# TensorE's expert loop at a given slot of an instruction-fetch block, with its far jumps announced

## The chip, the cores and the metric

One core of a Trainium2 chip runs the whole program. The metric is the device time of one execution in microseconds (us). Every core has five instruction streams (TensorE, VectorE, ScalarE, GpSimd, SyncE) that meet only at semaphores, and 16 DMA engines. A stream is fetched from memory in blocks while it runs; those fetches are DMA packets of their own, and the page of the profile lists them by queue as "instruction".

## The reference, cut to what matters

A decoder layer in float32: 256 tokens, 2048 channels. Attention, a gated mixer and an output projection come first. The part around the change is the second half, a mixture of 16 experts in 4 groups; every token goes to two experts of one group.

```python
    for e in range(N_EXPERTS):
        hid = jax.nn.silu(t @ w_gate[e]) * (t @ w_up[e])
        y = y + combine[:, e:e + 1] * (hid @ w_down[e])
```

How many tokens an expert gets is known only at run time.

## The kernel before

The program starts with the attention and mixer part, written out flat, up to about 850 us of the span. Then come the experts, four to a turn, in a loop of four turns. Each of TensorE, ScalarE, VectorE and SyncE has its own loop over the turns.

TensorE's turn: it gathers the tokens of the turn's four experts (64 places each) with matmuls of `hot` against `x1` (helper at line 924). Then, for each of the four experts `le`, it loads the expert's token count into a register (`value_load`, helper at line 1213) and asks whether it exceeds 64 (`br_cond`, line 628). If not, it goes on in the next instructions, the small body `pe{le}_few`. If so, it jumps to `pe{le}_more`, which lies behind the whole loop, asks again (line 640 and below) and runs one of three large bodies: `one_extra` (up to 96 tokens), `two_extra` (up to 128) or `all_extra`. The large body repeats the expert's work with further tiles of tokens: a gather of these tokens (line 741), turns (lines 694 and 756), gate and up products (line 675), down products (line 687) and sums (line 699). Its last instruction jumps back to `pe{le}_end` in the middle of the loop (lines 644, 651 and the one after). The large bodies are placed behind the loop in the order of the experts, each as a copy of its own.

Every float32 matmul of the source is four instructions of TensorE's stream (two weight loads, two matmuls; the profile counts the pairs). With that, the stream ahead of the loop has 7,175 instructions. Counted from the loop's first instruction as 0, the question of expert 0 is instruction 136, `pe0_end` begins at 553, `pe2_end` (where the count of the last expert is loaded) at 1466, the jump back is 1960, `pe0_more` is 1962, `one_extra` of expert 0 goes from 1963 to 3274, and its `two_extra` from 3276 to 5470, each with the jump out as its last instruction.

The weights of an expert are 12 transfers of 2048 KB. SyncE issues them in the order of use into seven places, each when TensorE's last matmul from that place is done (`half_multiplied` and `load_half`, lines 562 to 573). When all seven are full, the DMA engines stand still until TensorE frees one.

VectorE adds the results into `acc`; after the last expert it normalises, and SyncE stores the output.

Of the kernel before, what the change touches and what calls it, by code (L numbers as in the profile page):

```python
# [26 lines left out]
NE = 16  # L27
# [12 lines left out]
EXTRA = {1: (64, 32, 2), 2: (96, 32, 3), 3: (128, 64, 4), 4: (192, 64, 7)}  # L40
GRP = 4
# [43 lines left out]
def fills(n):  # L85

    return n // RING - sum(m <= n and m % RING == n % RING for m in ODD_ROWS)
# [46 lines left out]
def expert_at(g, le):  # L134

    return le % GRP * GRP + g + le // GRP
# [33 lines left out]

E_PLACES = 7
TURN_HALVES = 2 * GRP * E_UNITS

def place_of(t, h):

    return (2 * t + h) % TURN_HALVES % E_PLACES

LAST_USE = [max(range(i, TURN_HALVES, E_PLACES)) for i in range(E_PLACES)]

def uses(i):

    return len(range(i, TURN_HALVES, E_PLACES))

# [4 lines left out]
def program(nc, x_tok_d, x_T_d, c_T_d, rel_bias_d, router_w_d, router_b_d, ada_w_d, ada_b_d, ada_bT_d, w_in_d,  # L192
            sgu_g_d, sgu_b_d, sgu_wT_d, sgu_bias_d, w_branch_d, w_out_d, ln1_g_d, ln1_b_d, ln2_g_d, ln2_b_d,
            w_up_gate_d, w_down_d, square_d, slots_d, buckets_d, out_d):
    with ExitStack() as ctx:
# [227 lines left out]
        def e_half_loaded(eng, g, t, h):  # L423

            i, use = place_of(t, h), (2 * t + h) // E_PLACES
            before = 0 if i == E_PLACES - 1 else fills(NFRONT + i // 2) - 1
            eng.wait_ge(expert_landed(t, h), g * (16 * uses(i)) + 16 * (before + use + 1))

        def expert_half(t, h):

            i = place_of(t, h)
            if i == E_PLACES - 1:
                return region_g[:, :]
# [24 lines left out]
        def _(sp):  # L458
# [122 lines left out]
            with sp.Fori(0, NE // GRP - 1) as g:  # L581
                for i in range(E_PLACES, TURN_HALVES):
                    half_multiplied(g, (i - E_PLACES) // 2, (i - E_PLACES) % 2)
                    load_half(g, i // 2, i % 2)
                for i in (E_PLACES - 1, *range(E_PLACES - 1)):
                    half_multiplied(g, LAST_USE[i] // 2, LAST_USE[i] % 2)
                    load_half(g, GRP * E_UNITS + i // 2, i % 2)
            for i in range(E_PLACES, TURN_HALVES):
                half_multiplied(NE // GRP - 1, (i - E_PLACES) // 2, (i - E_PLACES) % 2)
# [32 lines left out]
                return four[c][:, a * 256:(a + 1) * 256]  # L622
            return four[2 * a + c][:, :]

        def few_tokens(eng, name, count, body):

            here = nc.cur_bb
            eng.br_cond(count > EXTRA[1][0], on_true=f"{name}_more", on_false=f"{name}_few")
            nc.switch_bb(f"{name}_few", parent=here)
            body(())  # L630
            eng.br(f"{name}_end")
            nc.switch_bb(f"{name}_end", parent=here)
            return here

        def more_tokens(eng, name, kind, count, here, body):

            more = nc.body(f"{name}_more", parent=here, valid_engines=[kind])
            with more:
                above = nc.cur_bb
                eng.br_cond(count > EXTRA[2][0], on_true=f"{name}_over_two", on_false=f"{name}_one_extra")  # L640
                nc.switch_bb(f"{name}_one_extra", parent=above)
                body((1,))
                eng.sem_inc(extra_end[kind], 1)
                eng.br(f"{name}_end")
                nc.switch_bb(f"{name}_over_two", parent=above)
                above = nc.cur_bb
                eng.br_cond(count > EXTRA[3][0], on_true=f"{name}_all_extra", on_false=f"{name}_two_extra")
                nc.switch_bb(f"{name}_two_extra", parent=above)
                body((1, 2))
                eng.sem_inc(extra_end[kind], 1)  # L650
                eng.br(f"{name}_end")
                nc.switch_bb(f"{name}_all_extra", parent=above)
                body((1, 2, 3, 4))
                eng.sem_inc(extra_end[kind], 1)
                eng.br(f"{name}_end")

        def bank_of(x, n):
            return psum[n] if x == 0 else psum[EXTRA[x][2]]
# [263 lines left out]
        def _(pe):  # L922
            def mm(out, lhsT, rhs, start, stop):
                return nc.tensor.matmul(out, lhsT, rhs, start=start, stop=stop)  # L924
# [270 lines left out]

            pe.wait_ge(routed, 1)
            with nc.Fori(0, NE // GRP, engines=[mybir.EngineType.PE], hint_back_edge=True) as g:

                pe.wait_ge(hot_ready, g + 1)  # L1200
                for m in range(KC // 2):
                    b = m % len(SUM_BANKS)

                    pe.wait_ge(m_taken[b], g * BANK_JOBS + m // len(SUM_BANKS) + 1)
                    for kk in range(2):
                        k = 2 * m + kk
                        for a in range(TT):
                            last = mm(psum[SUM_BANKS[b]][:, kk * T:(kk + 1) * T], x1[:, a, k * P:(k + 1) * P],
                                      hot[:, a, :, :].rearrange("p e s -> p (e s)"), a == 0, a == TT - 1)
                    last.then_inc(m_full[b], 1)  # L1210
                asked = []
                for le in range(GRP):
                    count = pe.value_load(counts[0:1, bass.ds(expert_at(g, le), 1)], min_val=0, max_val=T)
                    here = few_tokens(pe, f"pe{le}", count, lambda xs: expert_pe(pe, mm, g, le, xs))
                    asked.append((count, here))
            for le, (count, here) in enumerate(asked):
                more_tokens(pe, f"pe{le}", mybir.EngineType.PE, count, here, lambda xs: expert_pe(pe, mm, g, le, xs))

# [788 lines left out]
```

## Time and profile before

| | us |
|---|---|
| median of 3 runs | 1926.54 (1922.68 to 1928.22) |
| the profiled execution | 1924.21 |
| its span, first to last instruction | 1922.5 |
| TensorE matmuls busy | 1752.0 (91%) |
| DMA, mean rate over the span | 328 GB/s |
| VectorE busy | 508.8 (26%) |

The span is cut by turns: the flat part to 850, the first turn to 1142, the second to 1404, the third to 1639, the fourth to 1900, then the last normalisation. In a busy figure for TensorE a matmul that waits inside the array or runs at half clock counts as busy, so 91% doesn't say that TensorE is the limit everywhere. "issue" as the cause of idle time means that the engine waited for nothing that the profile shows: its own instruction stream hadn't delivered the next instruction. "GB/s" of a stretch shows whether the weights flow (428 is what they reach when nothing holds them) or stand.

### The profile page before, as it was taken

Reading aid. Unit: us, or ns where it says so; the run is one execution under the profiler, and the core shown is the slowest. Engines: PE = TensorE matmul, PEld = TensorE weight load, DVE = VectorE, ACT = ScalarE, POOL = GpSimd, SP = SyncE. Lnnn points to the kernel's source line nnn. Section 1 sums busy time; section 2 is a strip of 40 time slices with the busy share of each in tenths; the row PEclk is TensorE's granted clock in tenths of the full one; section 3 lists DMA queues with packets and bytes.
Section 4 is the critical chain, followed back from the end, with each engine's and each line's share of the span. In section 5 each row is a group of like instructions: output and inputs, shape, how many; then the busy total and the mean of one; then the engine's idle time right before and its main releaser. Section 6 shows DMA issues by size and latency. Waiting matters only on the chain.

```text
span 1922.5 us, 21633 instructions
## 1 busy us (share of the span) xinstructions
PE 1752.0 (91%) x8982; PEld 957.5 (50%) x8983; DVE 508.8 (26%) x944; ACT 163.5 (9%) x342; POOL 2.5 (0%) x9
## 2 busy tenths in 40 slices
PE   6889999999999999978989988899899888899994
PEld 3337888688888884454433243333243222432321
DVE  1441436655355101140121120111111111111114
ACT  0001013100000000041000011000020000200000
POOL 0000000000000000000000000000000000000000
PEclk9889999999999999989999998999999999999998
DMA  9996884687668624433779996899999999699995
GB/s 385 425 392 175 348 351 183 257 333 328 271 274 345 263 109 176 175 132 125 277 304 429 427 427 279 363 412 428 427 429 428 429 427 429 289 408 374 427 428 215
DMA packets 50993, 629.65 MB, mean 328 GB/s; under 512 B 5775, under 2 KB 8240, under 8 KB 11848
## 3 DMA queue, kind: packets, MB, share of 16 engines
q1 hardware_dynamic: 49768, 623.15, 78.2%
q10 hardware_dynamic: 1120, 5.00, 0.7%
q8 instruction: 78, 1.28, 0.3%
q14 instruction: 27, 0.22, 0.0%
HBM read 624.46 MB, written 3.67 MB: 327 GB/s over the span
## 4 chain that ended last, share of the span: by engine, by line
PE 76%; DMA 16%; DVE 3%; issue 2%; SPq 1%; ACT 1%; ACTq 0%; DVEq 0%
PE bank L924 42%; PE bank L675 20%; PE bank L687 9%; DMA ring<-in_w_down 8%; DMA ring<-in_w_up_gate 7%; PE bank L699 3%; DMA ring<-in_w_in 1%; DVE ada_rows L1534 1%; PE bank L694 1%; PE bank L741 1%; SPq L470 1%; PE bank L956 1%; ACT region_f L1226 0%; DVE region_a L1493 0%; SPq L463 0%
## 5 line engine op out<-in xcount | busy, mean ns | idle before, releaser
L675 PE MATMUL bank<-ring,region_b 128*64 128x512 f32 x1792 | 410.0, 606 | 39.5 <-DMA ring<-in_w_up_gate 18.5
L924 PE MATMUL bank<-region_a,ring 128*128 128x256 f32 x1792 | 390.3, 380 | 0.0
L924 PEld LDWEIGHTS bank<-region_a,ring 128*128 128x128 f32 x1792 | 340.1, 190 | 48.8 <-issue 3.8
L675 PEld LDWEIGHTS bank<-ring,region_b 128*64 128x64 f32 x1792 | 125.8, 139 | 298.3 <-issue 265.3
L687 PE MATMUL bank<-ring,region_f 128*64 128x512 f32 (+1 forms) x1408 | 231.0, 518 | 31.6 <-DMA ring<-in_w_down 25.1
L1534 DVE SCALAR_TENSOR_TENSOR ada_rows<-ring,condT,ada_rows 128x512 f32<-128x512 f32 x293 | 220.2, 752 | 10.2 <-DMA ring<-in_ada_w 0.3
L687 PEld LDWEIGHTS bank<-ring,region_f 128*64 128x64 f32 (+1 forms) x1408 | 78.3, 127 | 168.4 <-issue 121.8
L1855 DVE TENSOR_TENSOR region_a<-bank,region_a 128x512 f32<-128x512 f32 x128 | 79.5, 683 | 204.3 <-PE bank L699 202.9
L924 PE MATMUL bank<-ring,region_b 128*128 128x512 f32 x256 | 110.3, 593 | 1.3 <-issue 1.3
L924 PE MATMUL bank<-ring,region_a 128*128 128x512 f32 x160 | 76.0, 629 | 7.6 <-DMA ring<-in_w_in 6.8
L924 PEld LDWEIGHTS bank<-ring,region_b 128*128 128x128 f32 x256 | 48.5, 190 | 61.9 <-issue 61.9
L1860 DVE TENSOR_TENSOR sgu_wT<-bank,g2x 128x512 f32<-128x512 f32 x32 | 22.1, 691 | 207.7 <-PE bank L687 207.6
L1882 DVE TENSOR_TENSOR work<-work,bank 128x256 f32<-128x256 f32 x32 | 13.5, 421 | 230.5 <-ACT work L1275 230.5
L924 PE MATMUL bank<-region_f,ring 128*128 128x256 f32 x256 | 60.9, 393 | 3.0 <-DVE region_d L1632 3.0
L675 PE MATMUL bank<-region_g,region_b 128*64 128x512 f32 x256 | 58.1, 596 | 4.9 <-DMA region_g<-in_w_up_gate 4.9
L924 PE MATMUL bank<-region_e,region_x 128*128 128x256 f32 x256 | 58.1, 389 | 3.8 <-DVE region_e L1775 2.9
L924 PE MATMUL bank<-region_d,ring 128*128 128x256 f32 x256 | 57.9, 379 | 0.0
L1275 ACT ACTIVATE work<-bank 128x256 f32<-128x256 f32 x32 | 12.3, 383 | 521.1 <-PE bank L675 521.1
L924 PEld LDWEIGHTS bank<-region_e,region_x 128*128 128x128 f32 x256 | 49.7, 195 | 13.2 <-DVE region_a L1855 3.3
L924 PEld LDWEIGHTS bank<-region_f,ring 128*128 128x128 f32 x256 | 50.6, 199 | 10.9 <-issue 3.7
L924 PEld LDWEIGHTS bank<-ring,region_a 128*128 128x128 f32 x160 | 31.4, 203 | 45.3 <-issue 37.6
L924 PEld LDWEIGHTS bank<-region_d,ring 128*128 128x128 f32 x256 | 48.7, 190 | 6.6
(180 smaller groups left out, 862.3 us busy)
## 6 DMA issues: line engine op xcount, KB each, us to landing
ring<-in_w_up_gate SPq DMA_DIRECT2D x112, 2048.0 KB, 21.8
ring<-in_w_down SPq DMA_DIRECT2D x56, 2048.0 KB, 20.8
ring<-in_ada_w SPq DMA_DIRECT2D x44, 2048.0 KB, 11.8
ring<-in_w_in SPq DMA_DIRECT2D x31, 2048.0 KB, 16.3
region_g<-in_w_up_gate SPq DMA_DIRECT2D x16, 2048.0 KB, 22.5
ring<-in_w_branch SPq DMA_DIRECT2D x8, 2048.0 KB, 17.9
ring<-in_w_out SPq DMA_DIRECT2D x8, 2048.0 KB, 11.4
region_g<-in_w_down SPq DMA_DIRECT2D x8, 2048.0 KB, 21.8
```

The costliest lines, as they stand in the source:

```text
L470: sp.dma_start(dst[:, :, cols], w_in_d[first:first + width, :, cols].rearrange("u p n -> p u n"))\
L675: last = nc.tensor.matmul(bank_of(x, j)[n * c:n * c + n, 0:2 * m], tokens(x, 8 * half + k), w[:, k % 4, :, m * c:m * c + m], start=(half = ...
L687: last = nc.tensor.matmul(bank_of(x, q)[n * c:n * c + n, 0:m], hidT[x][:, k, :], w[:, k % 4, m * c:m * c + m], start=(k == 0), stop=(k == ...
L694: last = nc.tensor.transpose(psum[5][:, b * P:(b + 1) * P], src[:, b * P:(b + 1) * P], ident)
L699: return nc.tensor.matmul(bank, ones_t[n * c:n * c + n, a, :], y[n * c:n * c + n, :], start=True, stop=True, tile_position=(n * c, 0))
L741: last = nc.tensor.matmul(own[n * c:n * c + n, :], hotx[:, a, 0:n], x1[:, a, col:col + 512], start=(a == 0), stop=(a == TT - 1), tile_posi ...
L924: return nc.tensor.matmul(out, lhsT, rhs, start=start, stop=stop)
L956: last = nc.tensor.matmul(psum[6][32 * c:32 * c + 32, :], cond_pad[:, 32 * k:32 * k + 32], w[:, k, :], start=(k < 4), stop=(k >= KC - 4), ...
L1534: ins = dve.scalar_tensor_tensor(out=dst, in0=w[:, k, :], scalar=condT[:, k:k + 1], in1=dst, op0=ALU.mult, op1=ALU.add)
L1855: return dve.tensor_tensor(dst, bank[:, :], dst, ALU.add)
L1860: dve.tensor_tensor(ysb[q], psum[q][:, :], g2x[:, q * UW:(q + 1) * UW], ALU.mult)\
L1882: dve.tensor_tensor(hid[j], silu_g[j], psum[j][:, 256:512], ALU.mult).then_inc(hid_ready, 1)
```

## The change

A constant `LOOP_SLOT = 104` is added. In place of `Fori`, TensorE's loop is written by hand: a register counts the turns, an `addr_align` puts the instruction behind the next jump on slot 104 of a fetch block, and the back jump is a compare-and-branch. Five kinds of jump in TensorE's stream are announced: at the start of a turn the question of expert 0 (before, the back jump was announced there); at the start of each large body its jump out; ahead of loading the last expert's count the jump back. `few_tokens` takes the announcement of its question, and `leave` attaches one to the jump out. Other engines keep their code; matmuls, waits and their order stay.

```diff
+LOOP_SLOT = 104
...
+            jump = eng.br_cond(count > EXTRA[1][0], on_true=f"{name}_more", on_false=f"{name}_few")
+            if announced is not None:
+                jump.branch_hint(announced)
...
+        announcing = (mybir.EngineType.PE,)
+
+        def leave(eng, label, announced):
+
+            jump = eng.br(label)
+            if announced is not None:
+                jump.branch_hint(announced)
...
                 nc.switch_bb(f"{name}_one_extra", parent=above)
+                announced = eng.mark_branch_hint_location() if kind in announcing else None
                 body((1,))
                 eng.sem_inc(extra_end[kind], 1)
-                eng.br(f"{name}_end")
+                leave(eng, f"{name}_end", announced)
...
-            with nc.Fori(0, NE // GRP, engines=[mybir.EngineType.PE], hint_back_edge=True) as g:
+            kinds = [mybir.EngineType.PE]
+            turn_no = nc.alloc_registers("expert_turn", engines=kinds)
+            nc.regs_mov(turn_no, 0)
+            pe.addr_align(bass.FETCH_BLOCK_INSTRUCTIONS, offset=LOOP_SLOT, max_nops=0)
+            nc.br("pe_expert_turn", engines=kinds)
+            with nc.body("pe_expert_turn", valid_engines=kinds):
+                g = nc.snap(turn_no, min_val=0, max_val=NE // GRP - 1)
+                large_announced = pe.mark_branch_hint_location()
...
+                    if le == GRP - 1:
+                        back_announced = pe.mark_branch_hint_location()
...
+                nc.regs_alu(turn_no, turn_no, 1, op=mybir.AluOpType.add)
+                pe.br_lt(turn_no, NE // GRP, on_true="pe_expert_turn", on_false="pe_experts_end").branch_hint(back_announced)
+            nc.switch_bb("pe_experts_end")
```

The same announcement stands at the start of `two_extra` and `all_extra`.

## Rows read from the trace of the kernel before

**Rows 1.** The page: the chain that ended last, and the instruction packets of queue 8.

```profile
PE 76%; DMA 16%; DVE 3%; issue 2%; SPq 1%; ACT 1%; ACTq 0%; DVEq 0%
q8 instruction: 78, 1.28, 0.3%
```

**Rows 2.** Windows by turn: PE, PEld, DVE, ACT, POOL busy; clock, DMA share, GB/s.

```profile
850.00:1142.00 292.00, 265.30 (x1800) 105.82 (x1800) 49.84 (x108) 23.66 (x51) 0.00 (x0) 0.97 0.75 311
1142.00:1404.00 262.00, 237.32 (x1361) 89.66 (x1360) 41.03 (x83) 20.29 (x44) 0.00 (x0) 0.97 0.92 386
1404.00:1639.00 235.00, 206.99 (x921) 73.54 (x920) 32.58 (x66) 18.29 (x38) 0.00 (x0) 1.00 1.01 428
1639.00:1900.00 261.00, 236.22 (x1361) 89.38 (x1360) 40.08 (x75) 20.30 (x44) 0.00 (x0) 0.98 0.90 378
```

**Rows 3.** Waits of TensorE in 1404:1639 (us in total, times, longest).

```profile
PE bank L687 <- DMA ring<-in_w_down: 11.3, 10, 1.3
```

**Rows 4.** Timeline of TensorE, second turn, first matmuls of the large body.

```profile
1157.98 0.43 PE L694 MATMUL bank<-square,region_e 128*128 128x128 f32 x2 [1.39 <-ACT region_b L1447]
1159.16 0.14 PEld L741 LDWEIGHTS bank<-region_x,region_e 128*32 128x32 f32 x2 [0.98 <-issue]
1159.17 0.61 PE L741 MATMUL bank<-region_x,region_e 128*32 128x512 f32 x1 [0.75 <-ACT region_d L1266]
1165.80 3.64 PE L741 MATMUL bank<-region_x,region_e 128*32 128x512 f32 x15 [6.02 <-issue]
1169.36 4.08 PE L675 MATMUL bank<-ring,region_b 128*64 128x512 f32 x16
```

**Rows 5.** The same place in the fourth turn.

```profile
1662.28 3.35 PE L741 MATMUL bank<-region_x,region_e 128*32 128x512 f32 x15 [5.63 <-issue]
1665.55 3.65 PE L675 MATMUL bank<-ring,region_b 128*64 128x512 f32 x16
```

**Rows 6.** Timeline of TensorE, first turn, jumps into the large body.

```profile
873.19 0.61 PE L694 MATMUL bank<-square,region_e 128*128 128x128 f32 x2 [4.74 <-issue]
874.55 3.64 PE L741 MATMUL bank<-region_x,region_e 128*32 128x512 f32 x16 [0.75 <-ACT region_d L1266]
```

**Rows 7.** Timeline of TensorE at the jumps out: turns one, two, four.

```profile
981.80 5.70 PE L675 MATMUL bank<-ring,region_b 128*64 128x512 f32 x16 [5.46 <-issue]
...
1243.50 6.25 PE L675 MATMUL bank<-ring,region_b 128*64 128x512 f32 x16 [3.94 <-issue]
...
1739.28 5.35 PE L675 MATMUL bank<-ring,region_b 128*64 128x512 f32 x16 [3.96 <-issue]
```

**Rows 8.** Timeline of TensorE at a jump back, the one ahead of turn three.

```profile
1399.37 4.92 PE L699 MATMUL bank<-sgu_wT,ada_rows 64*128 64x512 f32 x16
1404.63 14.08 PE L924 MATMUL bank<-region_e,region_x 128*128 128x256 f32 x64 [0.35 <-issue]
```

**Rows 9.** Instruction packets (count, MB): 0:850, 1142:1150, 1238:1404, 1404:1658.

```profile
q8 instruction: 28, 0.46, 0.2%
...
q8 instruction: 1, 0.02, 0.8%
...
q8 instruction: 7, 0.11, 0.3%
...
q8 instruction: 1, 0.02, 0.0%
```

**Rows 10.** Windows: clock behind a stall; DMA around three exits and a body's start.

```profile
1166.00:1170.00 4.00, 4.00 (x17) 0.73 (x11) 0.00 (x0) 0.51 (x1) 0.00 (x0) 0.50 0.19 74
...
982.00:994.00 12.00, 12.00 (x46) 3.67 (x46) 2.49 (x6) 0.00 (x0) 0.00 (x0) 0.84 0.50 190
1244.00:1258.00 14.00, 14.00 (x54) 4.29 (x52) 2.48 (x4) 0.00 (x0) 0.00 (x0) 0.83 0.71 286
1741.00:1753.00 12.00, 12.00 (x52) 3.90 (x50) 2.48 (x4) 0.00 (x0) 0.00 (x0) 0.89 0.75 294
1166.00:1182.00 16.00, 16.00 (x133) 5.88 (x129) 1.38 (x2) 2.26 (x3) 0.00 (x0) 0.87 0.05 20
```

More of the change, by code:

```diff
@@ L623, in sum_bank, with few_tokens @@
             return four[2 * a + c][:, :]
-        def few_tokens(eng, name, count, body):
+        def few_tokens(eng, name, count, body, announced=None):
             here = nc.cur_bb
-            eng.br_cond(count > EXTRA[1][0], on_true=f"{name}_more", on_false=f"{name}_few")
+            jump = eng.br_cond(count > EXTRA[1][0], on_true=f"{name}_more", on_false=f"{name}_few")
+            if announced is not None:
+                jump.branch_hint(announced)
             nc.switch_bb(f"{name}_few", parent=here)
@@ L648, in more_tokens @@
                 nc.switch_bb(f"{name}_two_extra", parent=above)
+                announced = eng.mark_branch_hint_location() if kind in announcing else None
                 body((1, 2))
                 eng.sem_inc(extra_end[kind], 1)
-                eng.br(f"{name}_end")
+                leave(eng, f"{name}_end", announced)
                 nc.switch_bb(f"{name}_all_extra", parent=above)
+                announced = eng.mark_branch_hint_location() if kind in announcing else None
                 body((1, 2, 3, 4))
                 eng.sem_inc(extra_end[kind], 1)
-                eng.br(f"{name}_end")
+                leave(eng, f"{name}_end", announced)
         def bank_of(x, n):
@@ L1212, in _ @@
                 for le in range(GRP):
+                    if le == GRP - 1:
+                        back_announced = pe.mark_branch_hint_location()
                     count = pe.value_load(counts[0:1, bass.ds(expert_at(g, le), 1)], min_val=0, max_val=T)
-                    here = few_tokens(pe, f"pe{le}", count, lambda xs: expert_pe(pe, mm, g, le, xs))
+                    here = few_tokens(pe, f"pe{le}", count, lambda xs: expert_pe(pe, mm, g, le, xs),
+                                      large_announced if le == 0 else None)
                     asked.append((count, here))
+                nc.regs_alu(turn_no, turn_no, 1, op=mybir.AluOpType.add)
+                pe.br_lt(turn_no, NE // GRP, on_true="pe_expert_turn", on_false="pe_experts_end").branch_hint(back_announced)
+            nc.switch_bb("pe_experts_end")
             for le, (count, here) in enumerate(asked):
```

## The prediction

> **What bounds the kernel now.** Start at the chain of the page: TensorE has 76% of it, the DMA engines 16%, and "issue" 2% [rows 1]. Two per cent are small, but they are the only time that this change can touch, so I looked for where they lie. The windows by turn tell which engine sets the pace: in the third turn the weights flow at 428 GB/s, their full rate, and TensorE waits for them in small pieces (10 waits for the down weights, 11.3 us); in the first, second and fourth they flow at 311, 386 and 378 [rows 2, 3]. Those three turns have a large body for expert 0 (the timeline shows lines 741 and 694 there: `two_extra` in the first turn, `one_extra` in the second and fourth). In a large body TensorE is so slow with a set of weights that all seven places fill and the DMA engines stand: 20 GB/s in 1166:1182 [rows 10]. From there until the places empty again, a microsecond lost by TensorE is lost at the end; once the weights flow at full rate, TensorE's losses are covered by the waits for weights.
>
> The timeline of TensorE then shows the stalls by "issue" in those stretches: 4.74 us on the way into the first large body, 6.02 and 5.63 us inside the other two, and 5.46, 3.94 and 3.96 us at the three jumps out; at a jump back only 0.35 [rows 4 to 8]. [...]
>
> **What the stalls are.** The flat part has 7,175 instructions and 28 packets: 256 to a block [rows 9]. In the second turn 16 instructions of the large body run (three register or wait instructions, the two pairs of line 694 with their waits and registers, two weight loads and one matmul of line 741), then nothing for 6.02 us [rows 4]. So a block begins at instruction 1979 of the loop. 1979 + 69 = 2048 = 8 x 256: the loop's head now lies at slot 69, the loop fills eight blocks to slot 2029, and `pe0_more` with 16 instructions of the body is the tail of the eighth. The third turn needs one packet in 1404:1658 [rows 9], so at least eight blocks are kept. Behind the exit of turn two come 7 packets and then that one: all eight blocks anew, the head's among them, and still the jump back costs 0.35 us [rows 8, 9]. So the announcement works, and it works late: the head's block is asked for when the block with the announced jump is entered, in place of the block that follows. This is also why the body's second block is missing at instruction 1979: the armed word named the head. From asking to going on takes 5.6 to 6.0 us, by the two stalls inside the bodies.
>
> **Part by part.** New places: head at slot 104, one more instruction by then (the announcement ahead of the last expert), so the jump back is at 104 + 1961 = 2065, slot 17 of a ninth block, and `pe0_more` at slot 19 of it.
>
> 1. *The second block of the body.* It is now 236 instructions behind the jump in, and the next block is asked for on entering the ninth. The 6.02 and 5.63 us go. With them goes the half clock: the 15 gather matmuls take 3.64 and 3.35 us, about 1.8 at full clock, and line 675 has 4.08 against 3.65 in turn two: 2.2 and 1.5 us. DMA stands behind both [rows 10], so all of it counts: 8.2 + 7.1 = 15.3.
>
> 2. *The exits.* The jump out of `two_extra` lies 201 instructions behind its block's start: hidden. Of 5.46 us some 0.8 for loading the count remain, so 4.7 + 2.05 of clock = 6.75. In `one_extra` it lies 52 instructions behind the start of its block (of 1313, from slot 20). Those 52 run in about 4.4 us and are issued ahead, so of the 3.94 us some 0.8 remain; if nothing were issued ahead, 2.7. Middle: 3.1 + 2.6 = 5.7 and 3.1 + 1.7 = 4.8. But what comes next is the weights: they can gain only the time in which they stand around the exit, by the windows 12 x (1 - 190/428) = 6.7, 14 x (1 - 286/428) = 4.6 and 12 x (1 - 294/428) = 3.8 us [rows 10]. The exits give 6.7 + 4.6 + 3.8 = 15.1.
>
> 3. *The question at the turn's start.* It matters in the first turn alone: afterwards the ninth block is there from the turn before. Announced, the first of two fetches goes. Without that fetch the second starts while the gathers still run, and of 4.74 us about 1.6 remain (in turn two, with no fetch at all, 1.39 at this place [rows 4]): 3.1. On the way the ninth block's follower is asked for as well and may hold up the jump to `two_extra`, by nothing or by as much as the 3.1; no row shows which, and I take 0.8 off, nearer to nothing, because a fetch that nobody waits for needn't be first. Half clock: 16 matmuls in 3.64 us [rows 6] and the next ones, some 2.5. Together 4.8; between 0 (the jump lies in the block in which it is announced, which no row shows to work) and 5.6.
>
> 4. *The jump back.* It lies 17 instructions behind the ninth block's start. If the head's block is still there, 0 are lost. If not, it is asked for only then. The last instructions are issued while the 16 matmuls of line 699 run (4.92 us, to 1404.3) [rows 8]: asked for about 1400.3, there at 1406.2, 1.9 us lost; asked for only as its matmuls run (1402.4), 4.0. No row shows whether nine blocks are kept. I take 1.9, as issue runs ahead elsewhere too. Ahead of turn three it is hidden (weights flow on at 428); ahead of two and four it counts: 3.8. The bounds are 0 and, unannounced, 5.7 + 2.2 of clock each.
>
> [...]
>
> 5. *Added instructions*: an announcement per turn and body, once a jump over at most 255 empty slots ahead of the loop, which costs no more than a jump back does, 0.35 us [rows 8]. Nothing that counts. No queue of DMAs is moved.
>
> **Sum.** 15.3 + 15.1 + 4.8 - 3.8 = 31.4 us. Profiled execution: 1924.2 - 31.4 = 1892.8. The median of the runs lies 2.3 above that execution; I state 1893.
>
> **Rivals.**
> - *A jump back with no time to announce* (fetched at full price, 7.9 instead of 1.9 twice): 12 more, 1905. For it: only 17 instructions. Against: issue ahead. 0.14.
> - *The exits' announcements do nothing*, say because they hold only for a compare-and-branch, and what is announced here is an unconditional jump: 15.1 are missing, 1908. No row shows one announced. 0.12.
> - *None of the announcements acts* (the change doesn't do what it says) and only the place counts: bodies -15.3, two jumps back + 15.8: 1924.7, no change. Against: the announcement of before worked. 0.05.
> - *Slower: an announcement takes the turn of the block that follows it.* It stands just behind a block's start in every large body. Then the body's next block is missed again in turns two and four (no gain), newly in the first (+8.1), and the block behind the last expert's start four times at 8.1 less some 4.8, four waits for weights of 1.2 us [rows 3] that cover it (+13.2); the exits of turns two and four still gain 8.4 and the first question 4.8: +8.1, 1932. It decides once the dropped fetch costs more than the waits behind it. Against: at the head of turn two the announcement came at once behind a block's start and that block's follower was still fetched (1 packet in 1142:1150) [rows 9]. 0.05.
> - *Smaller gains by mixtures of these*: 0.09, between 1897 and 1918.
>
> **How the numbers follow.** My forecast has 0.55, with its own range 1886 (no loss at the jumps back, all of item 3, 1 us of noise) to 1900 (item 3 at nothing, exits at their lower end). To hold 8 in 10, the range takes in the first two rivals: 1885 to 1911. Faster by over 0.3% (5.8 us, about what a measurement can tell): 0.55 + 0.14 + 0.12 + 0.07 = 0.88; within: 0.07; slower: 0.05.
>
> **What would show it.** In the timeline of after: the 15 matmuls of line 741 follow the first without a gap (item 1); no gap over 1 us and 16 matmuls in 3.65 us behind each exit, and the weights' windows there near 428 (item 2); the gap ahead of line 694 in turn one at about 1.5 (item 3); gaps of about 2 us ahead of the gathers of turns two to four (item 4); and instruction packets in the third turn: one if nine blocks are kept, eight or nine if not. Wrong would be: a long gap at another instruction of a large body, or a half clock behind the jumps back.

## The result and the profile after

The changed kernel takes 1915.84 us (median; 1913.61 to 1919.88) where the kernel before takes 1927.26 beside it: ratio 0.9949, 95% interval 0.9936 to 0.9961. It is faster by some 10 us (0.0051 of 1927; the two medians differ by 11.4), where 31.4 were forecast, and outside the range of 1885 to 1911. The profiled execution of after takes 1914.61 us, its span is 1912.8; before had 1924.21 and 1922.5. In the code of after the lines have moved: 675 is now 689 (gate and up), 687 is 701 (down), 694 is 708, 699 is 713 (sums), 741 is 755 (the body's gather), 924 is 938 (the turn's gather), 640 is 651.

The page of after, its chain and its instruction packets [answers to rows 1]:

```profile
q8 instruction: 85, 1.39, 0.3%
...
PE 76%; DMA 16%; DVE 3%; issue 2%; SPq 1%; ACT 1%; ACTq 0%; DVEq 0%
```

Seven packets more, and still 2% "issue". The windows by turn, cut at the first gather matmul of each turn [rows 2]:

```profile
852.40:1140.10 287.70, 262.33 (x1801) 105.03 (x1801) 50.41 (x102) 22.38 (x50) 0.00 (x0) 0.98 0.78 326
1140.10:1399.20 259.10, 237.00 (x1361) 90.81 (x1361) 41.13 (x82) 20.28 (x44) 0.00 (x0) 0.97 0.92 389
1399.20:1639.60 240.40, 208.13 (x921) 74.67 (x921) 32.47 (x64) 18.29 (x38) 0.00 (x0) 0.99 0.99 420
1639.60:1900.00 260.40, 234.60 (x1360) 90.13 (x1360) 46.57 (x86) 20.87 (x46) 0.00 (x0) 0.98 0.88 368
```

For the same cut of before, the timeline of TensorE has its first gathers at these times (the third turn's is in [rows 8]):

```profile
852.57 1.64 PE L924 MATMUL bank<-region_e,region_x 128*128 128x256 f32 x3 [2.91 <-DVE region_e L1775]
...
1142.51 1.77 PE L924 MATMUL bank<-region_e,region_x 128*128 128x256 f32 x7 [0.34 <-issue]
...
1639.38 1.99 PE L924 MATMUL bank<-region_e,region_x 128*128 128x256 f32 x8 [0.20 <-issue]
```

From first gather to first gather, and in the fourth turn to TensorE's last sum (1899.45 before, 1889.98 after), the turns took 289.9, 262.1, 234.8 and 260.1 us; now they take 287.7, 259.1, 240.4 and 250.4. Three turns gained; the third, which has no large body, lost 5.6. The timeline of after tells why. These are the gathers ahead of turns two, three and four:

```profile
1140.10 2.50 PE L938 MATMUL bank<-region_e,region_x 128*128 128x256 f32 x5 [6.32 <-issue]
...
1399.17 2.07 PE L938 MATMUL bank<-region_e,region_x 128*128 128x256 f32 x4 [6.16 <-issue]
...
1639.57 6.80 PE L938 MATMUL bank<-region_e,region_x 128*128 128x256 f32 x19 [6.42 <-issue]
```

A jump back that cost 0.2 to 0.35 us now costs 6.2 to 6.4, all three times. The rest of the change did what it should. First the question of turn one and the first matmuls of the large bodies of turns two and four [rows 4 to 6], then the first matmuls behind the three exits [rows 7]:

```profile
871.56 0.43 PE L708 MATMUL bank<-square,region_e 128*128 128x128 f32 x2 [3.30 <-issue]
...
1159.83 3.60 PE L755 MATMUL bank<-region_x,region_e 128*32 128x512 f32 x16 [0.83 <-ACT region_d L1293]
...
1658.66 1.92 PE L755 MATMUL bank<-region_x,region_e 128*32 128x512 f32 x16 [0.75 <-ACT region_d L1293]
1660.52 3.65 PE L689 MATMUL bank<-ring,region_b 128*64 128x512 f32 x16
```

```profile
974.40 3.65 PE L689 MATMUL bank<-ring,region_b 128*64 128x512 f32 x16 [0.93 <-issue]
...
1232.95 3.60 PE L689 MATMUL bank<-ring,region_b 128*64 128x512 f32 x16
...
1730.11 3.60 PE L689 MATMUL bank<-ring,region_b 128*64 128x512 f32 x16
```

The 16 matmuls of line 755 run without a gap. In turn four they take 1.92 us; in turn two they take 3.60, at a granted clock of 0.53 in 1159.8:1163.4, so a half clock stands there still, without a stall ahead of it. Behind all three exits 16 matmuls take 3.60 to 3.65 us. Windows of after (clock, DMA share and GB/s are the last three columns): around the exits, behind the first jump back, and in the third turn:

```profile
975.00:987.00 12.00, 12.00 (x58) 4.00 (x56) 4.80 (x9) 0.00 (x0) 0.00 (x0) 1.00 0.99 400
1232.00:1246.00 14.00, 14.00 (x66) 4.62 (x64) 3.87 (x8) 0.00 (x0) 0.00 (x0) 1.00 1.00 421
1730.00:1742.00 12.00, 12.00 (x56) 3.90 (x54) 3.78 (x7) 0.00 (x0) 0.00 (x0) 1.00 1.00 417
...
1140.00:1143.00 3.00, 2.90 (x7) 2.37 (x8) 0.05 (x1) 0.00 (x0) 0.00 (x0) 0.50 1.01 423
...
1415.00:1425.00 10.00, 8.88 (x42) 3.18 (x44) 0.00 (x0) 2.06 (x3) 0.00 (x0) 1.00 0.60 233
```

Around the exits the weights flow at 400 to 421 GB/s where they had 190 to 294 [rows 10]. Behind the jump back the clock is 0.50. And the fifth window shows something that the prediction had excluded: in the third turn, some 16 us behind the stall, the weights fall to 233 GB/s for 10 us. Through the stall itself they flowed on (426 GB/s in 1133.5:1139.5 of the first jump back), so the places filled while TensorE emptied none. SyncE's waits for a free place there show it, after (1385:1430) and before (1404:1430), in total, times and longest:

```profile
SPq L574 <- PE bank L689: 36.2, 3, 30.6
...
SPq L573 <- PE bank L675: 26.1, 2, 23.3
```

Packets of queue 8 of after, in 866:869 and 1399:1640, and below them those of before in 866:870:

```profile
q8 instruction: 2, 0.03, 8.6%
...
q8 instruction: 9, 0.15, 0.2%
```

```profile
q8 instruction: 1, 0.02, 1.5%
```

Nine packets in the third turn, as many as the loop has blocks. Two packets at once at the first question: their share, 8.6% of 16 engines in 3 us, is 4.1 us, or 2.1 us for each, against 1.5% of 4 us, 0.96 us, for the single one of before.

### The profile page after: what moved, and what is told of

It is laid out like the page before. It is cut to its first block, busy times and chain, and to the rows that moved or that the text cites. A ratio compares the mean times of both kernels' runs of the same rounds, so it can differ in the third digit from the quotient of the medians.

```text
span 1912.8 us, 21645 instructions
## 1 busy us (share of the span) xinstructions
PE 1747.9 (91%) x8982; PEld 959.1 (50%) x8983; DVE 508.8 (27%) x944; ACT 163.4 (9%) x342; POOL 2.5 (0%) x9
## 4 chain that ended last, share of the span: by engine, by line
PE 76%; DMA 16%; DVE 3%; issue 2%; SPq 1%; ACT 1%; ACTq 0%; DVEq 0%
PE bank L938 42%; PE bank L689 20%; PE bank L701 9%; DMA ring<-in_w_down 8%; DMA ring<-in_w_up_gate 7%; PE bank L713 3%; DMA ring<-in_w_in 1%; DVE ada_rows L1561 1%; PE bank L708 1%; SPq L471 1%; PE bank L970 1%; PE bank L755 1%; ACT region_f L1253 0%; DVE region_a L1520 0%; SPq L464 0%
## 5 line engine op out<-in xcount | busy, mean ns | idle before, releaser
L689 PE MATMUL bank<-ring,region_b 128*64 128x512 f32 x1792 | 402.4, 596 | 30.6 <-DMA ring<-in_w_up_gate 22.1
L938 PE MATMUL bank<-region_e,region_x 128*128 128x256 f32 x256 | 65.0, 421 | 21.8 <-issue 18.9
L1909 DVE TENSOR_TENSOR work<-work,bank 128x256 f32<-128x256 f32 x32 | 13.5, 421 | 237.4 <-ACT work L1302 237.4
L938 PEld LDWEIGHTS bank<-region_e,region_x 128*128 128x128 f32 x256 | 54.5, 215 | 33.3 <-issue 24.4
## 6 DMA issues: line engine op xcount, KB each, us to landing
ring<-in_w_down SPq DMA_DIRECT2D x56, 2048.0 KB, 22.2
ring<-in_w_branch SPq DMA_DIRECT2D x8, 2048.0 KB, 18.2
region_g<-in_w_down SPq DMA_DIRECT2D x8, 2048.0 KB, 23.3
```

The source lines that it names most:

```text
L689: last = nc.tensor.matmul(bank_of(x, j)[n * c:n * c + n, 0:2 * m], tokens(x, 8 * half + k), w[:, k % 4, :, m * c:m * c + m], start=(half = ...
L1909: dve.tensor_tensor(hid[j], silu_g[j], psum[j][:, 256:512], ALU.mult).then_inc(hid_ready, 1)
```

## The experiments

Two theories stood at the beginning. Mine: an announced block is asked for on entering the block that holds the jump, and the jump back of after comes too soon behind that (slot 18 of the ninth block, counted in the program; the prediction had 17). The rival: the stall has another cause than the distance, such as a hand-written jump that is not served as the `Fori`'s was, or a ninth block that is too much. Positions below are slots of 256-instruction blocks: with the head at slot s, the jump back lies at s + 1962, the question of expert 0 at s + 137, the exits of `one_extra` and `two_extra` of expert 0 at s + 3277 and s + 5474.

**The head at slot 84**, where the jump back lies in the eighth block.

```diff
-LOOP_SLOT = 104
+LOOP_SLOT = 84
```

> The changed kernel with LOOP_SLOT = 84 instead of 104 and nothing else. The loop then ends with the jump back at slot 254 of its eighth block, and the first large body starts the ninth. In the changed kernel the gap ahead of the gathers of turns two to four is 6.2 us each and no packet is asked for between the start of the ninth block and the jump, 18 slots later. Theory 'too late': an announced block is asked for when the block with the jump is entered, and a jump that comes before the packet has gone out asks anew and pays the whole price; then the three gaps shrink to about 0.35 and the kernel gains about 5.8 us for each, so about 1897 to 1900. Theory 'without effect': the announcement ahead of the last expert does nothing wherever the jump lies; the head's block has been pushed out by the ninth, and the gaps stay at 6. By both the jump out of one_extra, now 33 slots behind its block's start instead of 53, may become a gap of up to 3.9 us again (1905 to 1908 in that case).

Measured: 1917.42 us (ratio 0.995, interval 0.9935 to 0.9965), no better than after. Ahead of turn three:

```profile
1399.00 1.22 PE L938 MATMUL bank<-region_e,region_x 128*128 128x256 f32 x2 [6.42 <-issue]
```

All three stalls stay, at 6.4 to 6.5 us, though the jump lies 254 slots behind its block's start. "Distance from the block's start" alone is therefore wrong or incomplete; the last experiment comes back to it.

**The head at slot 160**: the jump back at slot 74 of the ninth block.

```diff
-LOOP_SLOT = 104
+LOOP_SLOT = 160
```

> The changed kernel with LOOP_SLOT = 160: the jump back lies 74 slots behind the start of the ninth block, the loop still needs nine blocks. 'Too late': with 74 slots the head's block comes in time, and the gaps ahead of turns two to four fall from 6.2 to below 1 us, though nine blocks don't fit. 'Without effect': they stay at 6.2. A third theory, that nine blocks as such cost the time, also says 6.2. The second block of the large body is 184 slots behind its start: no gap there by any.

Measured: 1903.45 us. The first jump back, and the exit of `two_extra`:

```profile
1142.12 4.15 PE L938 MATMUL bank<-region_e,region_x 128*128 128x256 f32 x18 [0.47 <-issue]
```

```profile
980.79 3.68 PE L689 MATMUL bank<-ring,region_b 128*64 128x512 f32 x8 [4.56 <-issue]
```

The stalls at the jumps back are gone (0.47, 0.51 and 0.55 us), with the same hand-written loop of nine blocks. The rival falls. In exchange the exit of `two_extra`, now at slot 2 of its block, stalls for 4.56 us: announced, but with no room between the block's start and the jump. The same cause, made to appear at another jump.

**Without the announcement of the jump back.**

```diff
-                    if le == GRP - 1:
-                        back_announced = pe.mark_branch_hint_location()
...
-                pe.br_lt(turn_no, NE // GRP, on_true="pe_expert_turn", on_false="pe_experts_end").branch_hint(back_announced)
+                pe.br_lt(turn_no, NE // GRP, on_true="pe_expert_turn", on_false="pe_experts_end")
```

> The changed kernel without the announcement of the jump back, all else kept (slot 104). If that announcement brings nothing with the jump 18 slots into its block, this kernel equals the changed one: gaps of 6.2 us ahead of turns two to four, time within 2 us of it. If it brings a part (a fetch under way when the jump comes), the gaps grow to 7 us or more.

Measured: 1913.23 us in one execution, 0.4 below the lowest run of after: no slower for the missing announcement. The wait for the gather ahead of turn two:

```profile
1140.14 2.07 PE L938 MATMUL bank<-region_e,region_x 128*128 128x256 f32 x4 [6.22 <-issue]
```

6.22, 6.24 and 6.26 us without an announcement, 6.32, 6.16 and 6.42 with one. At slot 18 the announcement brought nothing at all, not a part of the time.

**The place alone**: the kernel before, its `Fori` and its single announcement at the head of the turn, with the head at slot 104.

```diff
-            with nc.Fori(0, NE // GRP, engines=[mybir.EngineType.PE], hint_back_edge=True) as g:
+            with nc.Fori(0, NE // GRP, engines=[mybir.EngineType.PE], hint_back_edge=True,
+                         head_slot={mybir.EngineType.PE: 104}) as g:
```

> The kernel before with its loop's head at slot 104 and nothing else: one announcement at the head of each turn, for the jump back; exits and questions unannounced. By the reading on which the prediction rests (an armed word names the head's block in place of the block that follows, whenever the jump's block is entered) the jump into the large body, which enters the ninth block, asks for the head's block and not for the body's second one: a gap of 5.6 to 6 us then stands some 235 instructions inside the body in turns two and four instead of 16 inside. If the body's second block is simply asked for too late in the kernel before (16 slots), there is no gap inside the body. The exits keep 5.5, 3.9 and 3.9 us, the jumps back get about 6.

Measured: 1933.56 us. Its timeline at the jump back into turn three, and in the large bodies of turns two and four:

```profile
1410.64 1.64 PE L924 MATMUL bank<-region_e,region_x 128*128 128x256 f32 x3 [6.25 <-issue]
...
1181.53 2.80 PE L675 MATMUL bank<-ring,region_c 128*32 128x256 f32 x48 [1.69 <-issue]
...
1684.54 5.78 PE L675 MATMUL bank<-ring,region_c 128*32 128x256 f32 x72 [1.95 <-issue]
```

The announcement of before, which had worked at slot 237 of the eighth block, fails at slot 16 of the ninth. So it is the place and not the hand-written loop. And inside the bodies the stall has moved to instruction 2200 of the loop, exactly the next start of a block (104 + 2200 = 9 x 256): an armed announcement still keeps the block that follows from being asked for. The stall is only 1.7 to 1.95 us there; that this is because more matmuls are queued ahead of it is my reading, not shown.

**The loop in eight blocks.** The head at slot 69, and the large bodies pushed to slot 40 of the ninth block, so that all announced jumps have room.

```diff
-LOOP_SLOT = 104
+LOOP_SLOT = 69
+BODY_SLOT = 40
...
             nc.switch_bb("pe_experts_end")
+            pe.addr_align(bass.FETCH_BLOCK_INSTRUCTIONS, offset=BODY_SLOT, max_nops=0)
```

> Head at slot 69, so that the loop ends in eight blocks and the jump back lies at slot 239 of the eighth; the large bodies begin at slot 40 of the ninth. Theory (an announced jump costs nothing if its block is entered some microseconds ahead of it): the head's block is asked for on entering the eighth block, no gap over 1 us ahead of the gathers of turns two to four (the kernel after: 6.31, 6.15, 6.42), no gap in the bodies and 0.9 us or none at the exits (they lie 74 and 223 instructions behind their blocks' starts); span about 1912.8 - 17.4 = 1895.4, median about 1897. Rival (a jump near the end of its block loses its announcement because what the sequencer reads ahead already needs the following block, as a jump at slot 254 did): the three gaps of 6.2 us stay, median about 1915.

Measured: 1894.87 us, ratio 0.9841, interval 0.9828 to 0.9854: the gain of some 31 us that was forecast, and the best of all kernels here. All waits of TensorE for "issue" from 850 on (us in total, times, longest), then the window that answers to 1415:1425 of after:

```profile
PE bank L709 <- issue: 3.0, 1, 3.0
PE bank L939 <- issue: 1.3, 3, 0.5
PE bank L690 <- issue: 0.9, 1, 0.9
```

```profile
1399.00:1409.00 10.00, 10.00 (x50) 3.48 (x48) 0.00 (x0) 0.56 (x1) 0.00 (x0) 1.00 1.00 424
```

The three gaps at the jumps back are 1.3 us together, and the weights flow on at the start of the third turn (that turn takes 236.6 us, against 234.8 before and 240.4 in after). The instruction packets of its third turn, 1383:1620:

```profile
q8 instruction: 9, 0.15, 0.3%
```

Nine again, though the loop fills eight blocks. One comes at 1386.3, ahead of the question, and fits the block of the large body that the question's announcement names: with it this loop, too, asks for nine blocks. The gain is therefore not one of fewer fetches; it comes from where the announced jumps lie.

**The head at slot 140**: the jump back at slot 54.

```diff
-LOOP_SLOT = 104
+LOOP_SLOT = 140
```

> The kernel after with the head at slot 140: the jump back lies at slot 54 of the ninth block instead of 18, one_extra's jump out at slot 89 and two_extra's at slot 238 of their blocks. Theory (too few instructions between the start of the jump's block and the jump): 54 instructions, all issued while matmuls are still queued, give the announcement its 3 to 4 us, gaps ahead of the gathers of turns two to four at most 1.5 us, exits without stall; median about 1898, range 1895 to 1903. Rival (it was not the distance but something else of slot 104): 1915, three gaps of over 5 us.

Measured: 1898.72 us (ratio 0.9862, interval 0.9845 to 0.9878). In the profiled execution the jumps into turns two and four take 0.5 us, the one into turn three has the full stall:

```profile
1390.26 3.35 PE L938 MATMUL bank<-region_e,region_x 128*128 128x256 f32 x7 [6.40 <-issue]
```

The same instructions, the same place, and one of three fails. So 54 slots are enough at times only. This kernel also gives the price of a single stall ahead of the third turn. Some 16 us behind it the weights stand for 5 of 10 us:

```profile
1406.00:1416.00 10.00, 8.66 (x42) 3.06 (x44) 0.00 (x0) 2.28 (x3) 0.00 (x0) 1.00 0.58 216
```

and the profiled execution is 4.9 us above the kernel in eight blocks (1897.29 against 1892.43; by the ratios 4.0). The two kernels differ in the places of the other jumps too, but those are served in both.

**Exits not announced.**

```diff
-                announced = eng.mark_branch_hint_location() if kind in announcing else None
+                announced = None
```

> The kernel after without the announcements at the starts of the large bodies, so that the jumps out are not announced; all else stays. My step 2 says that they are worth 15.1 us: gaps of 5.5, 4.0 and 4.0 us behind the bodies come back, each with a half clock, and the median is about 1931. Rival (the weights cover more of it than the windows say, or the exits gain less beside the new fetches at the jumps back): 1922 to 1926.

Measured: 1929.09 us, ratio 1.0019 (1.0007 to 1.003). The three exits:

```profile
980.84 5.47 PE L687 MATMUL bank<-ring,region_b 128*64 128x512 f32 x16 [5.68 <-issue]
...
1241.72 6.43 PE L687 MATMUL bank<-ring,region_b 128*64 128x512 f32 x16 [4.04 <-issue]
...
1744.79 5.35 PE L687 MATMUL bank<-ring,region_b 128*64 128x512 f32 x16 [4.46 <-issue]
```

The stalls of before are back, with their slow matmuls. Against after (0.9949) the exits' announcements are worth 0.0070 of 1926, or 13.5 us, give or take some 3; 15.1 were forecast. By turns (first gather to first gather) they are 6.9, 3.1, 0.8 and 3.6 us. Of the 6.9 some 1.6 were already lost ahead of the exit, in the gathers and behind the question, where the granted clock was lower for longer than in after (0.83 against 0.88 over the gathers); the exit itself is about 5.3.

**The question not announced.**

```diff
-                large_announced = pe.mark_branch_hint_location()
...
-                                      large_announced if le == 0 else None)
+                                      None)
```

> The kernel after without the announcement of expert 0's question at the head of the turn. Theory (the announcement takes away the first of two fetches; the second, of two_extra's block, now shares its time with the follower of the first): the jump to the large body waits about 3 to 4 us and the next one again, the gap ahead of line 708's matmul in turn one is 4.5 us or more instead of 3.29, plus half clock, and the run is 2 to 4 us over the kernel after. Rival (the announcement does nothing for the question, and the 3.29 come from the second fetch alone): the gap stays at 3.3 and the time within 1 us.

Measured: 1921.12 us in one execution. The first question:

```profile
875.82 0.68 PE L708 MATMUL bank<-square,region_e 128*128 128x128 f32 x2 [6.16 <-issue]
```

6.16 us where after has 3.30, and 6.8 us of half clock behind it instead of 3.4. The announcement acts, at a jump in the very block in which it is made. But the same wait was 4.74 us in the kernel before [rows 6], unannounced: the new place makes it 1.4 us longer. What else this execution lost (2 to 3 us in turns two and four, whose instructions are the same) can't be told from the spread of the runs.

**The head at slot 76**: the jump back at slot 246 of the eighth block, `one_extra`'s exit 25 slots behind its block's start.

```diff
-LOOP_SLOT = 104
+LOOP_SLOT = 76
```

> The kernel after with the head at slot 76: the jump back lies at slot 246 of the eighth block, between the two places known so far (239: no stall, 254: full stall); one_extra's jump out lies 25 instructions behind its block's start (between 18, where the announcement of the jump back brought nothing, and 33, where an exit had no stall). Theory (only a jump within the last few slots of its block is lost): gaps ahead of the gathers of turns two to four under 1 us, exits of turns two and four hidden or at most 2 us; about 1897 if both hold. Rival (the sequencer reads on past the jump by some ten instructions and needs the ninth block): three gaps of 6.2 us, about 1914. If only the exits of one_extra fail: two gaps of 4 us, about 1905.

Measured: 1921.16 us (ratio 0.997, interval 0.9953 to 0.9987), some 4 us slower than after by the ratios. The three stalls of the jumps back are there (7.02, 6.89 and 7.29 us, 21.2 together against 18.9 in after; the one into turn three below), and none at `one_extra`'s exits.

```profile
1401.20 3.35 PE L938 MATMUL bank<-region_e,region_x 128*128 128x256 f32 x7 [6.89 <-issue]
```

**The head at slot 120**: the jump back at slot 34 of the ninth block, the question at slot 1 of the second.

```diff
-LOOP_SLOT = 104
+LOOP_SLOT = 120
```

> The kernel after with the head at slot 120: the jump back lies at slot 34 of the ninth block (18: three full stalls; 54: one of three; 74: none); one_extra's jump out is at slot 69, two_extra's at 218, and the question of expert 0 is at slot 1 of the second block of the loop. Theory (the announced block is asked for only if the sequencer still has some tens of instructions to the jump when it enters the block): all or most of the three gaps of 6.2 us stay, about 1912 to 1916; and the announced question, one slot behind a block's start, brings nothing, so that the gap in turn one is about 6 us instead of 3.3. Rival (34 is enough in the loop as 33 was at the exit of one_extra): gaps under 2 us, about 1898 to 1901.

Measured: 1905.22 us, with a wide spread, 1900.98 to 1920.49 (ratio 0.9905, interval 0.9872 to 0.9937). The first question and the three jumps back:

```profile
876.20 0.68 PE L708 MATMUL bank<-square,region_e 128*128 128x128 f32 x2 [6.83 <-issue]
...
1139.10 3.07 PE L938 MATMUL bank<-region_e,region_x 128*128 128x256 f32 x13 [0.50 <-issue]
...
1393.49 2.92 PE L938 MATMUL bank<-region_e,region_x 128*128 128x256 f32 x6 [6.34 <-issue]
...
1630.01 2.21 PE L938 MATMUL bank<-region_e,region_x 128*128 128x256 f32 x9 [2.68 <-issue]
```

None, all and a part of the stall, in this order, at the same jump. The question, one slot behind a block's start, has the full 6.8 us. Neither theory had said that the outcome would vary within one execution.

**Only the exits announced**, in the kernel before.

```diff
+                announced = eng.mark_branch_hint_location() if kind == mybir.EngineType.PE else None
                 body((1,))
                 eng.sem_inc(extra_end[kind], 1)
-                eng.br(f"{name}_end")
+                leave(eng, f"{name}_end", announced)
```

> The kernel before with its loop and its announcement of the jump back at the head of the turn, and only the exits of the large bodies announced. Theory A (one announcement is held at a time, and a new one replaces it): a turn with a large body loses the announcement of the jump back, so the gaps ahead of the gathers of turns two and three are about 6.2 us (before: 0.34, 0.35) and the one into turn four stays at 0.2; the exit of the first turn has no stall (before 5.46), those of turns two and four lie some 16 instructions behind their block's start and keep their 3.9; the second block of the bodies is still missed (6.0, 5.6). About 1924 - 6.7 + 13 = 1930. Rival B (several are held): the jumps back stay at 0.35, the first exit gains, about 1917.

Measured: 1925.76 us in one execution. Its gathers ahead of turns two, three and four:

```profile
1143.15 3.35 PE L933 MATMUL bank<-region_e,region_x 128*128 128x256 f32 x7 [6.26 <-issue]
...
1405.08 3.35 PE L933 MATMUL bank<-region_e,region_x 128*128 128x256 f32 x7 [5.78 <-issue]
...
1640.98 3.28 PE L933 MATMUL bank<-region_e,region_x 128*128 128x256 f32 x14 [0.17 <-issue]
```

Only one announcement is held. The two turns with a large body replace that of the jump back and stall; the third has no large body and keeps it. A jump out of `two_extra` is free (0.88 us), those out of `one_extra`, now 16 slots behind their block's start, keep 3.94 and 4.01 us. That the time hardly moves has a reason that I hadn't written down: with the jump back no longer armed at the end of turn one, the block behind the loop's last one, the body's second, is fetched there (one packet in 1103:1105, long ahead of the jump) and is still present in turn two. So its 6.02 us go as well (of the bodies' stalls only one is left, 5.2 us, in turn four), and the two new stalls eat both gains. That it stayed from turn one is read from the packets' times; no run tests it.

**Eight blocks again, the jump back at slot 246.**

```diff
-LOOP_SLOT = 69
+LOOP_SLOT = 76
 BODY_SLOT = 40
```

> The kernel of e5_loop_in_8_blocks with the head at slot 76 instead of 69 and nothing else changed; the large bodies stay at slot 40 of the ninth block, and the jump back moves from slot 239 to 246 of the eighth. If the place of the jump alone decides, the three gaps of 6.2 to 7.3 us ahead of the gathers of turns two to four are back and the run takes about 1894.9 + 18 = 1913; if it was something else of slot 76 or 84, it stays at 1895. The end of the loop tells which block is fetched on entering the eighth: the jump behind the last turn goes to slot 40 of the ninth. Theory A (the announcement isn't taken up, and the follower, the ninth block, is fetched): that jump goes through at once. Theory B (the head's block is fetched, and the ninth is asked for later because the sequencer reads past the jump): it waits some 3.5 us, as it does in e5_loop_in_8_blocks (3.52).

Measured: 1916.43 us in one execution. Its waits for the gathers:

```profile
PE bank L939 <- issue: 21.1, 3, 7.1
```

Seven slots make 20 us of stalls: 239 works and 246 doesn't. The jump behind the last turn, which goes to slot 40 of the ninth block, takes 0.32 us here and 3.52 in the kernel with slot 69. So on entering the eighth block the ninth was fetched: theory A, the announcement is not taken up. Theory B, a sequencer that takes up the announcement and then asks for the ninth block as well, is out. Why seven slots decide it stays open.

## Why the prediction was wrong

**Item 1, the body's second block: right.** Both stalls are gone. Of their half clocks one remains in after, at line 755 in turn two (3.60 us for 16 matmuls, against 1.92 in turn four and, in both turns, in the kernel with eight blocks): 1.7 us. In the kernel with eight blocks turn two takes 248.6 us and turn four 248.1, where before had 262.1 and 260.1: 13.5 and 12.0 us, against 12.8 and 10.9 forecast for items 1 and 2 together.

**Item 2, the exits: right, and nearly so in size.** 13.5 us measured, give or take 3, where 15.1 were forecast. The cap by the standing weights fits: the three windows went from 190, 286 and 294 GB/s to 400, 421 and 417. The 2.05, 2.6 and 1.7 us "of clock" in this item are the first 16 matmuls behind the three exits [rows 7] less the 3.65 us of [rows 5]; the granted clock there was 0.50, 0.50 and 0.66 (981:985, 1243:1247 and 1739:1743 of before).

**Item 3, the first question: the right mechanism, too large.** 4.8 us forecast. The gap fell from 4.74 to 3.30, by 1.4 where 3.1 less 0.8 were forecast; the half clock behind it fell from 6.8 to 3.4 us, worth some 1.3 where 2.5 were forecast. From the first gather to the end of TensorE's work ahead of the exit the turn is 2.7 us shorter than before (121.1 against 123.8 us), and that is what item 3 gave. It fits the turn: 2.2 us gained although about 6.0 were lost at its jump back, 8.2 by the rest, of which the exit is about 5.5. Two terms were mis-sized. One is the 0.8 us taken off for the ninth block's follower, "because a fetch that nobody waits for needn't be first". The two packets run side by side and take 2.1 us each instead of 0.96; the kernel in which the question is unannounced shows the price, 6.16 against 4.74 us, or 1.4. That before had no follower here because the armed jump back displaced it fits the packets (one at a time there, three in 865:880). The other is the 2.5 of clock, which supposed that no half clock would be left.

**Item 4, the jump back: wrong, and with it the time.** 3.8 us forecast for two jumps; what three cost is the difference of two kernels that differ in seven slots, 1916.4 - 1892.4 (both profiled executions) = 24.0 us, or 8.0 on average. In after the gaps are 0.7 us shorter each, so about 22, and after stands 22.2 us above the kernel in eight blocks (1914.61 - 1892.43). They don't cost the same: the one ahead of turn three costs 4 to 5 us by the kernel with the head at slot 140, so that the other two must be dearer than 8.0, if the prices add up. Two steps of this item failed:

- "If not, it is asked for only then", on entering the ninth block, and 1.9 us of stall remain as issue runs ahead. With 18 instructions between the block's start and the jump nothing was asked for ahead: no instruction packet comes in 1133.5:1137 of after, one comes in 1137:1139, 3.7 us behind the jump, and the stall is as long with the announcement as without. That a served announcement acts on entering the block was right: in the kernel in eight blocks the packet comes in 1100:1103, and none in 1103:1137 up to and over the jump. No row of before showed how much room it needs; I took the value near the good end of bounds that reached from 0 to 5.7 + 2.2.
- "Ahead of turn three it is hidden (weights flow on at 428)". It isn't: in the third turn TensorE waits for weights [rows 3] and SyncE for places (23.3 us at the longest before): the places are close to full there. A stall of 6 us fills them (30.6 us), and the transfers then stand (233 GB/s in 1415:1425, 4.6 us of 10). A stall of TensorE was free there only as far as there were empty places.

**The sum again.** 31.4, less 18.2 at the jumps back (22 instead of 3.8), less 2.1 in item 3 (2.7 instead of 4.8), less 1.6 in item 2, is 9.5; the profiled executions differ by 9.6 and the ratio says 9.8 us. With 3 us of doubt in item 2 alone, so close a match is luck, but the order is clear: the jumps back are over four fifths of what is missing. The rival "a jump back with no time to announce" was the right one. Its 1905 fell short by the jump ahead of turn three (4 to 5 us, hidden by assumption), by items 2 and 3, and by the price of the other two. It is luck, too, that the kernel in eight blocks gains just the 31 us of the forecast: it hardly has the 3.8 at the jumps back, so by the items it should have gained 35.2.

**How many blocks are kept.** The 3.8 us of item 4 suppose that the head's block is gone at every jump back, and no row of before shows a loop of nine blocks. After does: its third turn has nine packets, where before had one, and a packet comes 3.6 to 3.9 us behind each of its three jumps back. So nine blocks were not all kept. The packets don't tell what that costs: the kernel in eight blocks has nine in the third turn as well, and its gaps at the jumps back are under 0.5 us. Nor is the block fetched ahead always the one that follows: an announced block is fetched in its place (the gaps of 1.69 and 1.95 us at instruction 2200 with only the place changed).

**The list of what would show it**: no gap in line 755, no long gap and 3.65 us behind the exits, weights near 428, and nine packets in the third turn were met. A gap of 1.5 us at the question and gaps of 2 us ahead of the gathers were not, and "a half clock behind the jumps back", named there as a sign of error, is what the trace shows.

## What to carry to other kernels

An announced jump needs a place, not only an announcement: here 74 to 239 slots behind the start of its fetch block. A step that rests on "some time is enough" should be costed at the full stall until a row shows otherwise. Lay out the loop so that every announced jump has that room; whether a loop of eight blocks is better than one of nine, once its jumps are served, no run shows (with the head at slot 160 a loop of nine blocks has gaps of 0.5 us and a third turn of 236.5 us, as the one in eight blocks has). And before a stall is called hidden behind transfers, ask whether the buffers have room to go on filling while the consumer stands.

## What the runs showed of the hardware

- **Where an announced jump must lie.** Slots of the 256 of the jump's block, where the announcement came earlier than that block. Served each time (gaps of 0.2 to 0.9 us, or none): 25 and 33 (exits of `one_extra` at head slots 76 and 84), 53 (the same in after), the exits between 69 and 238, and 74, 237 and 239 (jumps back). Served at times: 34 (jumps back: 0.50, 6.34 and 2.68 us) and 54 (two of 0.5 us, one of 6.40). Not served: 1 (question, 6.83 us), 2 and 16 (exits, 4.56 and 3.9 to 4.0 us), 16, 17 and 18 (jumps back, 5.9 to 6.5 us; at 17 one of three came 3.7 us early in the kernel without the question's announcement), 246 and 254 (jumps back, 6.4 to 7.3 us). Most of these places are known from one execution each. Why 25 suffices at an exit while 34 and 54 fail at times at the jump back, what makes it vary, and where between 239 and 246 the upper end lies, stays open.
- **One announcement is held.** A later one replaces it (6.26 and 5.78 us at the jumps back when the exits are announced as well). Where it is served, the block behind the jump's block is not fetched ahead (6.02 us inside the body before); where the jump lies at slot 246, the block behind is fetched instead (0.32 us against 3.52 at the end of the loop). Made in the jump's own block it acts at once: in after a packet comes in 851:853, 1.1 us behind it (850.7, 851.8).
- **The price of a fetch that was not asked for depends on the other transfers.** With the DMA engines standing the packet starts 1.1 us behind the jump and the jump takes 3.3 us (first question of before); with weights flowing it starts 3.6 to 3.9 us behind the jump, and the jump takes 6.1 to 6.4 us (jumps back of after). The half clock behind it adds 1.5 to 3.0 us to the 64 gather matmuls (15.55 to 17.07 us against 14.08). Of all this 4 to 5 us are left at the end for a single stall ahead of turn three, and 8.0 on average for the three.
- **Two packets at once cost double**: 2.1 us each against 0.96, and the wait behind them is 1.4 us longer (6.16 against 4.74).
